# Attention pairs moved in among the projection groups, and an earlier branch with a two-part gather in the expert dispatch

## What is computed

```python
def hierarchical_moe(h, ...):                  # 4 groups of 8 experts
    group_probs = softmax(t @ w_rg + b_rg)
    p_group, g_idx = top_k(group_probs, 1)     # each token picks one group
    in_group = exp_logits[token, g_idx]
    p_exp, e_idx = top_k(softmax(in_group), 2) # and two experts in it
    weights = p_group * p_exp / sum(p_exp)
    ...
    act = silu(t @ w_g) * (t @ w_u)
    out = out + (act * combine) @ w_d

def hybrid_mixer(h, ...):
    qa, ka, va, qb, kb, vb = split(h @ w_in + b_in)
    ya = swa_attention(qa, ka, va, sinks, ...) # 8 heads, window 128, 2 key heads
    yb = moba_attention(qb, kb, vb, ...)       # 8 heads, one block of 256 keys
    y = concatenate([rmsnorm(ya), rmsnorm(yb)])
    return y @ w_out
```

## Time and profile before

| | |
|---|---|
| median of 3 runs | 2398.7 us (2396.86 to 2399.32) |
| the profiled execution | 2397.78 us, its span 2396.0 us |
| PE busy | 2171.5 us, 91% |
| DVE busy | 1625.8 us, 68% |
| ACT busy | 1003.8 us, 42% |
| POOL busy | 83.8 us, 3% |
| mean granted PE clock | 0.946 |
| dispatch, layer 0, from the last output projection to the first expert | 227.4 to 280.1 us |
| the same, layer 1 | 754.0 to 808.6 us |
| attention, layer 0, projections and pairs | 1355.3 to 1470.6 us |
| the same, layer 1 | 1989.4 to 2107.9 us |

### The profile page before, as it was taken

How to read it: one execution, slowest core, us unless ns; L and a number is a source line. 1 busy time by engine, 2 the same in 40 slices (tenths; PEclk the granted TensorE clock), 3 DMA queues, 4 the chain that set the end, 5 groups by cost and what they waited for, 6 DMA issues and landing times.

```text
span 2396.0 us, 33191 instructions
## 1 busy us (share of the span) xinstructions
PE 2171.5 (91%) x12723; PEld 1918.4 (80%) x12723; DVE 1625.8 (68%) x2169; ACT 1003.8 (42%) x1444; POOL 83.8 (3%) x143
## 2 busy tenths in 40 slices
PE   4999899997999899996999898899969998978997
PEld 2787688886888688885999776789969996667997
DVE  5897699996995799995788415565458872337543
ACT  0121487775021578774333313334433341224443
POOL 0100000000100000000000001000000000100000
PEclk8999799999998899998999999899989998898998
DMA  7949398885768398884699520676248983024730
GB/s 271 342 168 346 131 374 344 337 344 191 263 232 338 130 374 338 343 325 160 217 326 336 180 88 6 241 264 206 76 138 309 337 274 106 18 87 145 246 103 18
DMA packets 252024, 543.40 MB, mean 227 GB/s; under 512 B 14290, under 2 KB 172524, under 8 KB 227308
## 3 DMA queue, kind: packets, MB, share of 16 engines
q1 hardware_dynamic: 251852, 541.50, 62.5%
q10 hardware_dynamic: 32, 0.02, 0.0%
HBM read 540.42 MB, written 1.07 MB: 226 GB/s over the span
## 4 chain that ended last, share of the span: by engine, by line
PE 74%; DVE 16%; issue 3%; DMA 3%; ACT 2%; SPq 1%; POOL 1%; DVEq 0%; ACTq 0%
PE ps L586 11%; PE ps L619 9%; PE ps L621 9%; PE ps L620 9%; PE ps L680 4%; PE ps L682 4%; PE ps L681 4%; DVE acc L1465 4%; PE ps L598 4%; DVE arena L1594 3%; PE ps L1113 3%; PE ps L720 2%; PE ps L722 2%; PE ps L721 2%; DVE ring_lo L1742 2%
## 5 line engine op out<-in xcount | busy, mean ns | idle before, releaser
L1742 DVE TENSOR_TENSOR ring_lo<-ring,wsg 128x1024 fp32r<-128x1024 f32 x384 | 459.9, 1224 | 45.1 <-ACT wsg L1232 40.7
L1505 DVE TENSOR_TENSOR wsp<-ring,wsp 128x1024 fp32r<-128x1024 f32 x264 | 321.6, 1224 | 217.5 <-ACT wsp L1188 210.7
L1232 ACT ACTIVATE wsg<-ring 128x1024 fp32r<-128x1024 f32 x384 | 405.5, 1059 | 79.2 <-PE ps L682 54.5
L619 PE MATMUL ps<-hsp,wsp 128*128 128x256 f32 x1408 | 407.2, 289 | 33.3 <-DVE hsp L1526 18.6
L1188 ACT ACTIVATE wsp<-ring 128x1024 fp32r<-128x1024 f32 x264 | 277.4, 1056 | 370.6 <-PE ps L621 324.8
L620 PE MATMUL ps<-hsp,wsp 128*128 128x256 f32 x1408 | 403.9, 287 | 0.0
L621 PE MATMUL ps<-hsp,wsp 128*128 128x256 f32 x1408 | 403.8, 287 | 0.0
L586 PE MATMUL ps<-arena,ring 128*128 128x256 f32 (+1 forms) x1760 | 378.8, 382 | 6.0 <-PE ps L586 5.2
L586 PEld LDWEIGHTS ps<-arena,ring 128*128 128x128 f32 (+1 forms) x1760 | 317.3, 184 | 61.2 <-issue 9.4
L619 PEld LDWEIGHTS ps<-hsp,wsp 128*128 128x128 f32 x1408 | 275.2, 195 | 36.6 <-DVE wsp L1505 20.9
L620 PEld LDWEIGHTS ps<-hsp,wsp 128*128 128x128 f32 x1408 | 275.1, 195 | 0.0
(11 more groups left out here) (217 smaller groups left out, 2799.4 us busy)
## 6 DMA issues: line engine op xcount, KB each, us to landing
ring<-in_w_expert_gate_dram SPq DMA_DIRECT2D x64, 1024.0 KB, 6.9
ring<-in_w_expert_up_dram SPq DMA_DIRECT2D x64, 1024.0 KB, 8.9
ring<-in_w_expert_down_dram SPq DMA_DIRECT2D x64, 1024.0 KB, 5.0
ring<-in_ada_w_dram SPq DMA_DIRECT2D x48, 1152.0 KB, 8.9
ring<-in_ffn_w_gate_dram SPq DMA_DIRECT2D x44, 1024.0 KB, 11.0
ring<-in_ffn_w_up_dram SPq DMA_DIRECT2D x44, 1024.0 KB, 13.3
ring<-in_ffn_w_down_dram SPq DMA_DIRECT2D x44, 1024.0 KB, 5.3
ring<-in_w_ada_dram SPq DMA_DIRECT2D x32, 1152.0 KB, 11.3
```

Source lines behind the costliest of these rows:

```text
L619: mm(dst, hi, v_hi, start=start, stop=False, skip_group_check=True)
L1232: act_(high_piece(n % HIGHS, j), piece(EXPERT_1[e], j), ACT.Identity).then_inc(S.whi, 1)
L1505: v_.tensor_tensor(split_part(at % SPLITS, 1, n), piece(unit, n), split_part(at % SPLITS, 0, n, F32), ALU.subtract).then_inc(S.wlo, 1)
L1742: v_.tensor_tensor(low_piece(EXPERT_1[e], j), piece(EXPERT_1[e], j), high_piece(n % HIGHS, j, F32), ALU.subtract).then_inc(S.wlo, 1)
```

## The change

**Dispatch.** PE's `sum_squares` goes ahead of the last two `ahead_later`, DVE's `keep_ahead` behind `normalize`. The router's matmuls run over the two token halves within each channel tile. The rank takes four matmuls for five. `S.route` is signalled right after `most` is written; a new `S.gsel` follows the matrix of window 0, and that of window 1 is built only on the long way. The tokens are split once: ACT rounds `htok` to `hth`, DVE subtracts to get `htl`, both in front of the rest of the routing. The gather multiplies each with `gsel_r` in float32r, high and low into two banks, so that two channel tiles fit in four banks. ACT copies all high results and five low ones (`LOW_BY_ACT`), DVE the last three low ones. On the short way ACT rounds two weight pieces and DVE makes one low piece before the gather's copies; ACT's second exponential and table load stand behind those two pieces.

**Attention.** Pairs 0 to 3 are worked through between the column groups of m1 and m2, each step some group after the one that it needs; the order of the groups kb and qb changes, the PSUM banks with it. `pt` moves to another place. Pairs 4 to 7 follow.

The 64 and 16 matmuls of the groups stand in pieces of 16 or 8, with steps of a pair between them. The core of the diff:

```diff
+                sum_squares(1, bank=6)
                 ahead_later(1)
                 ahead_later(2)
                 pe.wait_ge(S.ada_mod, units_in(7))
-                sum_squares(1, bank=6)
...
+                        pe.wait_ge(S.gsel, w + 1)
...
+                        pe.wait_ge(S.hth, TH)
+                        pe.wait_ge(S.htl, TH)
                         for k in range(KD):
                             n = w * KD + k
-                            if n >= 4:
-                                pe.wait_ge(S.gathl if nw == 1 else S.gath, n - 3)
...
+                            elif nw == 1 and k >= 2:
+
+                                pe.wait_ge(S.gath, highs_read(k - 2))
+                                if k - 2 >= LOW_BY_ACT:
+                                    pe.wait_ge(S.gathl, k - 2 - LOW_BY_ACT + 1)
+                            for part, src in enumerate((hth, htl)):
+                                dst = ps[:, 2 * (k % 2) + part if nw == 1 else k % 4, :]
...
+                    wait_landed(pe, 1, l, m1)
+                    pair(3, m1, 0, 0)
+                    ada_sum(8, 0, 7)
+                    evicted(S.qk, 3)
+                    scores(0)
+                    pair(0, m1, 2, 0)
+                    scores(1)
+                    turn_pair(0)
+                    pair(1, m1, 1, 0)
+                    evicted(S.vv, 1)
+                    value_pair(0)
+                    scores(2)
+                    turn_pair(1)
+                    pe.wait_ge(S.mm, 6)
+                    release(pe, m1)
+                    wait_landed(pe, 1, l, m2)
+                    evicted(S.qk, 4)
+                    pair(3, m2, 0, 0)
+                    value_pair(1)
+                    scores(3)
+                    turn_pair(2)
+                    values(0)
+                    value_pair(2)
+                    scores(4)
+                    turn_pair(3)
+                    values(1)
+                    pe.wait_ge(S.mm, 9)
+                    release(pe, m2)
+                    value_pair(3)
+                    scores(5)
                     evicted(S.qk, 7)
...
+                    scores(6)
+                    turn_pair(4)
+                    scores(7)
+                    value_pair(4)
+                    turn_pair(5)
+                    value_pair(5)
+                    turn_pair(6)
+                    value_pair(6)
+                    turn_pair(7)
+                    value_pair(7)
...
-                own(v_.tensor_copy(most[0:1, 0:1], rt[0:1, 296:297]))
+                v_.tensor_copy(most[0:1, 0:1], rt[0:1, 296:297]).then_inc(S.route, 1)
...
+                select(0)
+                for hf in range(TH):
+                    eng.wait_ge(S.hth, hf + 1)
+                    v_.tensor_tensor(htl[:, hf, :], htok[:, hf, :], hth[:, hf, :].bitcast(F32), ALU.subtract
+                                     ).then_inc(S.htl, 1)
...
+                    add_values(0)
+                    front(4)
+                    turned(3)
+                    sums(4)
+                    add_values(1)
+                    front(5)
+                    front(6)
+                    turned(4)
+                    sums(5)
+                    front(7)
+                    sums(6)
+                    turned(5)
+                    sums(7)
+                    turned(6)
+                    turned(7)
```

More of the change, by code:

```diff
@@ new lines, in values, with scores @@
+                    def values(hf):
+                        evicted(S.qk, 5 + hf)
+                        project(ps[:, hf, :], lambda k: h[:, k, hf * P:(hf + 1) * P],
+                                lambda k: w3(m2)[:, 1:3, k, :]).then_inc(S.mm, 1)
+                    def scores(i):
+                        if i == 5:
+                            evicted(S.vv, 3)
+                        elif i:
+                            pe.wait_ge(S.sc, i if i < 5 else i - 1)
+                        for a in range(2):
+                            q, k, _ = head(2 * i + a)
+                            bank = SCORE_BANK[i] + a
+                            mm(ps[:, bank, 0:T], q[:, P:T], k, start=True, stop=True)
+                            last = mm(ps[:, bank, T:384], q[:, 0:P], k[:, 0:P], start=True, stop=True)
+                        last.then_inc(S.S, 1)
@@ new lines, in turn_pair @@
+                    def turn_pair(t):
+                        pe.wait_ge(S.p, t + 1)
+                        if t == 0:
+                            pe.wait_ge(S.ada_mod, units_in(11))
+                        else:
+                            pe.wait_ge(S.pt, t)
+                        for a in range(2):
+                            for n, at in enumerate((T, 0, P)):
+                                last = mm(ps[:, 6 + a, n * P:(n + 1) * P], sc[:, t % 4, a, at:at + P], ident[:],
+                                          start=True, stop=True)
+                        last.then_inc(S.T, 1)
@@ L1314, in _, with second_exp @@
                 act_(rt[:, 80:88], rt[:, 72:80], ACT.Exp).then_inc(S.lexp, 1)
-                eng.wait_ge(S.log, 2)
-                act_(rt[:, 90:92], rt[:, 88:90], ACT.Exp).then_inc(S.lexp, 1)
-                table(ACT.Silu)
+                eng.wait_ge(S.ht, 4)
+                for hf in range(TH):
+                    act_(hth[:, hf, :], htok[:, hf, :], ACT.Identity).then_inc(S.hth, 1)
+                def second_exp():
+                    eng.wait_ge(S.log, 2)
+                    act_(rt[:, 90:92], rt[:, 88:90], ACT.Exp).then_inc(S.lexp, 1)
+                    table(ACT.Silu)
                 eng.wait_ge(S.route, 1)
@@ L1325, in _ @@
                 with eng.Else():
+                    experts(l, 1, early=True)
+                    second_exp()
                     gather(1)
@@ new lines, in result @@
+                    def result(t):
+                        eng.wait_ge(S.pv, t + 1)
+                        act_(yT[:, t, :], ps[:, VALUE_BANK[t], 0:T], ACT.Identity).then_inc(S.y, 1)
+                    for n in range(4):
+                        evict(n)
+                    eng.wait_ge(small[1], (l + 1) * (16 * SMALL_2))
+                    softmax(0)
+                    evict(4)
+                    softmax(1)
+                    evict(5)
+                    result(0)
+                    softmax(2)
@@ L1432, in _ @@
+                    evict(6)
+                    result(1)
+                    softmax(3)
+                    result(2)
+                    softmax(4)
+                    result(3)
+                    softmax(5)
+                    softmax(6)
+                    result(4)
+                    softmax(7)
+                    table(ACT.Sqrt)
+                    for t in range(5, PAIRS):
+                        result(t)
                     squares(lambda k: yT[:, k, :], S.y, 1)
@@ new lines, in _ @@
+                    for t in range(4):
+                        front(t)
+                        if t:
+                            turned(t - 1)
+                        sums(t)
+                    add_values(0)
[9 more added lines that the diff above has]
+                    sums(6)
```

274 lines of the change are left out of this document (122 added, 152 removed).

## The result

The changed kernel takes 2357.5 us in the median (2355.3 to 2358.3, 4 runs), the kernel before 2399.0 in the same runs: ratio 0.983, 95% interval 0.982 to 0.984. The forecast was 2361, with 2351 to 2378 as the range. The total is near; the terms are not. The dispatch gave more than forecast, the attention almost nothing, and some 6 us came from a stage whose code is the same. One execution of the kernel before, of 6654 us, counts as slow and is left out of all comparisons; the others lay between 2389 and 2405 us.

A forecast was written before the change was run, and what follows sets the result against it. PE was taken to pace the experts' stage and to wait or run at half clock in the changed stretches. Squares 10.1, dispatch 15.4 and attention 12.3 sum to 37.8; 2398.7 less that is 2361 us, range 2351 to 2378.

The forecast's parts named there:

- Squares first, 4.2 and 5.9: Ahead of the router: squares before the modulation sums end 4.2 us earlier in layer 0, 5.9 in layer 1.
- Router and rank matmuls, 0.43: Before the branch: reordered router matmuls give nothing, one rank matmul of five less gives 0.43 us.
- a case better than all bounds: Whole time below every bound, for one by router matmuls at full clock; chance 0.07.
- the middle, 4.4, is what I carry over: Dispatch: signal to PE's first matmul behind the branch, 4.7 and 4.1 us before, taken as 4.4 after the change.
- the earlier signal does nothing: Rival on the dispatch branch: gather starts no sooner, 2 x 3.9 us back, 2369; chance 0.05.
- PE and ACT are behind the branch at 255.7: Dispatch, layer 0: signal at 251.3 plus 4.4 us puts both engines behind the branch, nearly 4 us sooner.
- the 5.1 of the prediction: Gather: low bound of the 7.7 us by which the first expert is fed sooner, if half clock stays throughout.
- Attention groups, +16.2 + 0.5: Attention: steps moved between the column groups add 16.2 us, extra hand-overs 0.5, no wait counted.
- the slower rival: Attention: groups run at half clock, 35 us more per layer, 70 in all, 2431; chance 0.02.
- Tail, 20.2: Attention: from the last group to the squares takes 20.2 us, worked out at full clock.
- 12.3: Attention's whole gain over two layers: 6.0 us in layer 0 and 6.4 in layer 1.
- Experts giving it back: Rival: the experts' stage ends when it ended, the dispatch gain is lost, 2386; chance 0.05.

The follow-up runs named there:

- e7: The kernel before with one edit, PE's sum of squares moved ahead as in the change; 2389.6 us against 2398.9, ratio 0.996.
- after: The changed kernel itself, with the dispatch and attention parts together, against the kernel before; 2357.5 us, ratio 0.983.
- e5: The changed kernel with 23 matmuls of constants put into PE's waits in attention's tail; 2345.7 us, ratio 0.979.
- e3: The changed kernel with the branch signal given later, behind the first half of the selection matrices; 2356.0 us, ratio 0.982.
- e11: e5 with the second 12 one-column matmuls ahead of the router moved behind the rank matmuls; 2345.2 us, ratio 0.9791.
- e4: The changed kernel with the fourth expert weight unit requested behind the branch instead of ahead of it; 2354.8 us, ratio 0.982.
- e2: The kernel before with the attention part of the change alone, dispatch as before; 2388.5 us, ratio 0.996.
- e9: e5 with four more matmuls of constants ahead of the router's matmuls; 2345.3 us, ratio 0.9785.

## Why the prediction was right, and where it was not

**Squares first, 4.2 and 5.9: right.** In e7 the router starts 4.4 and 6.1 us sooner, and the whole time is 9.3 less.

**Router and rank matmuls, 0.43: mis-sized** where the clock stays up for a part of the router. From the router's start to the count it was 12.7 and 12.9 us and is 10.0 in after, 2.7 and 2.8 less; with a half-clock router (e5) it is 12.4, and 0.3 to 0.4 less. "The router's reordered matmuls pass the weight port at the same rate as before" left out that the clock may still be full when the router starts. It was in after, e3 and one layer of e11, not in e7, so it is no sure gain of the squares' place. The text had it as a case better than all bounds.

**The branch, "the middle, 4.4, is what I carry over": wrong** by 3.0 and 2.3. From the count to PE's start it was 7.9 and 7.3 us and is 7.4 and 6.7: the earlier signal gave 0.5 and 0.6, not 3.5. The 4.4 was read where the weights' stream had just ended; the change moved the fetch into the stream. That is near to the rival "the earlier signal does nothing", by a mechanism that it did not name.

**"PE and ACT are behind the branch at 255.7": wrong for ACT,** and this gave the gain back. ACT was through its branch within 2.5 us of the signal, and had its weight pieces and its table done by 254.1, so that the start of the gather did not wait for it. Its copies set the pace only further on, as forecast for the full clock. From PE's start to the first expert it took 13.1 and 13.2 us, not the forecast's 16.8; before 20.5 and 21.1. In layer 0 some 1.4 of the 3.7 us are the wait ahead of tile 2 that did not come (261.1 to 262.5 in the sum), and 1.3 are the clock: tiles 2 and 3 took 2.1 us (257.84 to 259.90), where the sum had 3.4 at half clock. e4 says that the reading of ACT's chain was sound for the case that it assumed: once PE's branch took 5.1, PE did wait for ACT. The two errors nearly cancel: 3.0 lost, 3.7 won. That transposes keep the clock down for the whole of a gappy gather, the 5.1 of the prediction, did not happen: the clock was up some 4.7 us after PE's start, within the fourth row of the gather. The Trainium skill, "TensorE: Matmul & The Clock Gate", section "Part 4: PE-mode transpose", speaks of the transposes alone; that the matmuls behind them would stay at half was the prediction's own step.

**Attention groups, +16.2 + 0.5: right,** 16.1 and no wait of over 0.6 us. It holds where the clock is full. In five of the 18 passes with this order (e2, e3 twice, e4, e9) the groups took 91.4 to 92.8 us in place of 88.5: their first product ran at half clock in whole or in part, and in four of them the clock was at half for 3.4 us more among the groups, in e2 from 1394.8. So the half clock in the groups, which the slower rival has, did occur, for a few us at a time.

**Tail, 20.2: the step that failed.** It was worked out at full clock, with the clock's 3 us only in the low bound. It took 25.5 and 25.6, because the clock fell while PE waited; the squares behind it took 1.7 more each. Of the 6.4 us won in the attention by the table, 2.8 are the start of layer 1's attention, 5.8 us in before and 3.0 in after; without them and with the slow squares next to nothing is left of 12.3. With the clock held (e5) the term is there: 5.8 us in layer 0, 7.3 in layer 1 without that start. The row that I rested on, a clock of 1.00 with PE busy 12.2 of 15 us, was a milder mix than the tail's 2.8 of 6. The steps of the sum had such waits in them, PE for DVE's copies, but no price for them in clock.

**Experts giving it back, slower groups: no.** PE's gain went through the experts' stage whole (301.9 to 300.2 us in layer 0, 296.8 to 296.9 in layer 1).

**Not in the sum at all:** the 6.4 us of the second feed-forward blocks. The forecast came out 3.5 us too high, and that it came so near is luck: terms that were not in it made up for the attention's. Of the two profiles' 40.6 us against the sum's 37.8, the dispatch gave 6.8 more and this stage 6.4; the attention gave 5.9 less, the stretch behind it took 2.5 and the rest 2.0.

## What to carry over

Draining a pipeline leaves PE waiting on one chain of engines: work out what that tail costs at half clock too, and where banks are free fill its waits with matmuls of constants (0.13 us a row here); here that was worth 12 us of 2357, as much as the reordering was meant to give. A branch's price is not a constant: it holds a fetch that queues with whatever stream of weights runs at that moment, so an earlier signal can buy almost nothing. And compare unchanged stages first: here they moved by 6 us with their code untouched.

## What had not been expected of the hardware

- PE's start behind a taken branch came 4.1 to 5.1 us after the signal with idle DMA engines, 5.8 to 7.4 us with the weights' stream running (6.7 to 7.4 in after, at 422 GB/s); ACT's and DVE's branches at the same place took at most 2.5 and 1.3 us.
- The same stretch of the same code ran at full clock or at half in different kernels and executions: the router 5.4 or 7.0 us, the start of the attention 3.0 or 5.8, the second feed-forward block 215.4 or 218.7, unfilled tails 20.6 once and 24.0 to 25.7 seven times.
- Of four edits meant to hold the clock two did so (filled tail, one-column matmuls apart) and two did not (filling and thinning ahead of the router). A fall that has already happened was not undone by four added matmuls.
